# Splitting the output weights inside the attention and moving loads into the projection of a hybrid encoder layer

## What is computed

```python
h += concat(rmsnorm(y_a, g_out_a), rmsnorm(y_b, g_out_b)) @ w_out   # the mixer
h += softmax(q k^T) v @ w_xo      # q from rmsnorm(h), k and v from 256 memory rows each, w_xkv
h += hierarchical_moe(rmsnorm(h)) # 32 experts, top-1 group, top-2 experts
y  = rmsnorm(h) * g_final
```

## Time and profile before

| | |
|---|---|
| time, three runs | 1410.42 us median (1410.22 to 1417.36) |
| profiled execution | 1412.83 us, its span 1411.2 us |
| busy share of the span | TensorE 86%, VectorE 46%, ScalarE 31%, GpSimd 17% |
| granted clock, mean | 0.932 |
| chain that ended last | TensorE 73%, DMA 7%, VectorE 7%, SyncE's queue 5% |

### The profile page before, as it was taken

How to read it: one execution, slowest core, us unless ns; L and a number is a source line. 1 busy time by engine, 2 the same in 40 slices (tenths; PEclk the granted TensorE clock), 3 DMA queues, 4 the chain that set the end, 5 groups by cost and what they waited for, 6 DMA issues and landing times.

```text
span 1411.2 us, 17465 instructions
## 1 busy us (share of the span) xinstructions
PE 1208.6 (86%) x5959; PEld 938.8 (67%) x5959; DVE 647.9 (46%) x1158; ACT 437.1 (31%) x893; POOL 237.3 (17%) x350
## 2 busy tenths in 40 slices
PE   4999999599998995999989979999973998899910
PEld 3888888488877884788854445658762886667600
DVE  4433222421126775433332064435467786665257
ACT  4322222400024553211111133323110765554222
POOL 0211111100012220000000000000022352223234
PEclk9999999799999998999989999999985999999965
DMA  7211111233166114533210100004145899999676
GB/s 234 70 59 54 59 59 30 66 75 76 30 138 183 27 24 143 179 88 89 59 60 0 59 1 15 16 16 135 45 132 177 292 333 314 337 338 332 189 281 257
DMA packets 167885, 178.91 MB, mean 127 GB/s; under 512 B 39054, under 2 KB 131214, under 8 KB 167822
## 3 DMA queue, kind: packets, MB, share of 16 engines
q1 hardware_dynamic: 150350, 140.33, 33.3%
q0 software_dynamic: 13824, 31.48, 6.2%
q10 hardware_dynamic: 3648, 6.29, 1.5%
HBM read 150.48 MB, written 42.51 MB: 137 GB/s over the span
## 4 chain that ended last, share of the span: by engine, by line
PE 73%; DMA 7%; DVE 7%; SPq 5%; issue 4%; ACT 3%; POOL 1%; ACTq 0%; POOLq 0%; DVEq 0%
PE bank L420 14%; PE bank L422 13%; PE bank L421 13%; PE bank L1698 13%; PE bank L1602 3%; PE bank L1778 3%; DMA at<-in_w_exp_down 3%; PE bank L1582 3%; PE bank L1591 2%; PE bank L1744 2%; PE bank L1764 1%; PE bank L1537 1%; PE bank L1658 1%; PE bank L1707 1%; DVE at L1481 1%
## 5 line engine op out<-in xcount | busy, mean ns | idle before, releaser
L420 PE MATMUL bank<-at,at 128*128 128x512 f32 (+1 forms) x1024 | 389.5, 380 | 27.2 <-DVE at L415 17.3
L422 PE MATMUL bank<-at,at 128*128 128x512 f32 (+1 forms) x1024 | 378.6, 370 | 0.0
L421 PE MATMUL bank<-at,at 128*128 128x512 f32 (+1 forms) x1024 | 378.3, 369 | 0.0
L415 DVE TENSOR_TENSOR at<-at,at 128x1024 fp32r<-128x1024 f32 (+2 forms) x106 | 156.9, 1484 | 182.9 <-ACT at L410 170.9
L420 PEld LDWEIGHTS bank<-at,at 128*128 128x128 f32 x1024 | 199.3, 195 | 61.2 <-DVE at L415 21.3
L422 PEld LDWEIGHTS bank<-at,at 128*128 128x128 f32 x1024 | 198.4, 194 | 31.8
L421 PEld LDWEIGHTS bank<-at,at 128*128 128x128 f32 x1024 | 199.6, 195 | 29.5
L1698 PE MATMUL bank<-at,at 128*128 128x512 f32 (+1 forms) x560 | 186.2, 491 | 6.0 <-DVE at L1222 3.3
L410 ACT ACTIVATE at<-at 128x1024 fp32r<-128x1024 f32 (+3 forms) x106 | 130.4, 1266 | 135.7 <-DMA at<-in_w_exp_down 38.9
L1698 PEld LDWEIGHTS bank<-at,at 128*128 128x128 f32 x560 | 93.6, 195 | 91.1 <-issue 86.3
L688 POOL TENSOR_TENSOR at<-at 128x1 f32<-128x1 f32 x88 | 27.9, 317 | 724.9 <-ACT at L980 332.9
(11 more groups left out here) (168 smaller groups left out, 1302.6 us busy)
## 6 DMA issues: line engine op xcount, KB each, us to landing
at<-in_w_exp_gate SPq DMA_DIRECT2D x39, 512.0 KB
at<-in_w_exp_up SPq DMA_DIRECT2D x39, 512.0 KB
at<-in_w_exp_down SPq DMA_DIRECT2D x39, 512.0 KB
at<-y_tok SPq DMA_DIRECT2D x24, 512.0 KB, 9.2
at<-y_mix SPq DMA_DIRECT2D x12, 512.0 KB, 4.5
xn_moe<-at SPq DMA_DIRECT2D x12, 512.0 KB, 2.6
at<-in_w_in SPq DMA_DIRECT2D x2, 2048.0 KB, 12.2
at<-in_x_sample POOLq DMA_DIRECT2D x8, 512.0 KB, 3.9
```

Of the source, the lines that this page charges most:

```text
L415: nc.vector.tensor_tensor(lo, x, hi.bitcast(F32), ALU.subtract).then_inc(lo_made, 1)
L420: nc.tensor.matmul(out, w_hi, x_hi, start=(k == 0), stop=False)
L421: nc.tensor.matmul(out, w_lo, x_hi, start=False, stop=False)
L422: last = nc.tensor.matmul(out, w_hi, x_lo, start=False, stop=(k == len(terms) - 1))
```

## The change

Three things are moved.

1. w_out is split in 16 pieces of 128 x 512, eight within steps of pair 1 (first half) and eight within steps of pair 3 (second half). Before pair 1 ScalarE waits for all 16 pieces of w_out. The buffers are laid out anew for it.
2. The rows of tiles 0 and 1 are loaded in pair 3 after the store of its third group, in place of the end. Their squares, their scaling, the transposes of tile 0 and their evacuation are put into the last steps of that pair. The last pair is written out in every stream.
3. The rows of tiles 2 and 3 are loaded right after the last stores. The k half of w_xkv (2 MB) is issued between the rows of tiles 3 and 4, its v half between those of 5 and 6, the memory rows between 7 and 8, and the router weights behind w_xq at the end of the projection.

```diff
@@ sync @@
             for g in range(NKG):
                 store_group(0, g)
                 for part in range(3 * g, min(3 * g + 3, 2 * KT)):
                     load_w_out(part)
...
-            for g in range(NKG - 1):
-                store_group(NPAIR - 1, g)
+            for g in range(3):
+                store_group(NPAIR - 1, g)
             for j in range(2):
                 sp.wait_ge(ya_stored[j], 16 * 2 * NT // 2)
             sp.wait_ge(na_stored[0], 32 * (3 * (NPAIR - 1) + 1))
-            sp.wait_ge(s_biased, 2 * NPAIR * NSTEP)
             for j in range(2):
-                load_rows(0, j, a["x_prompt"][0][0:GTOK])
-            store_group(NPAIR - 1, NKG - 1)
+                load_rows(0, j)
+            for g in range(3, NKG):
+                store_group(NPAIR - 1, g)
             for j in range(2):
                 sp.wait_ge(na_stored[j], 16 * 2 * NPAIR * NKG // 2)
-            sp.dma_start(w_xkv, a["w_xkv"][0].rearrange("(k p) n -> p k n", p=P)).then_inc(w_kv_rt_xo_here, 16)
-            sp.dma_start(w_rt[:, :, 0:NG], a["w_router_group"][0].rearrange("(k p) n -> p k n", p=P)).then_inc(w_kv_rt_xo_here, 16)
-            sp.dma_start(w_rt[:, :, NG:], a["w_router_expert"][0].rearrange("(k p) n -> p k n", p=P)).then_inc(w_kv_rt_xo_here, 16)
+            for j in range(2):
+                load_rows(1, j)
+            sp.dma_start(w_xk, w_xkv[:, :, 0:HALF]).then_inc(w_kv_xo_here, 16)
+            for j in range(2):
+                load_rows(2, j)
+            sp.dma_start(w_xv, w_xkv[:, :, HALF:]).then_inc(w_kv_xo_here, 16)
+            for j in range(2):
+                load_rows(3, j)
             for n, rows in enumerate((a["mem_prompt"][0], a["mem_sample"][0])):
                 for j in range(2):
                     sp.dma_start(mem_in[2 * n + j], rows[j * P:(j + 1) * P]).then_inc(mem_here[j], 16)
-            for j in range(2):
-                load_rows(1, j, a["x_prompt"][0][GTOK:2 * GTOK])
-            with sp.Fori(2, NT // 2) as i:
+            for i in range(4, NT // 2):
+                for j in range(2):
+                    load_rows(i, j)
             sp.wait_ge(wo_done, NT)
+            sp.dma_start(w_xq, a["w_xq"][0].rearrange("(k p) n -> p k n", p=P)).then_inc(w_xq_rt_here, 16)
+            sp.dma_start(w_rt[:, :, 0:NG], a["w_router_group"][0].rearrange("(k p) n -> p k n", p=P)).then_inc(w_xq_rt_here, 16)
+            sp.dma_start(w_rt[:, :, NG:], a["w_router_expert"][0].rearrange("(k p) n -> p k n", p=P)).then_inc(w_xq_rt_here, 16)
@@ scalar @@
                     if s >= 1:
                         evac_pT(s - 1)
+                    if hp in (1, NPAIR - 1) and s < KT:
+                        n = int(hp == NPAIR - 1)
+                        make_hi(act, split_w_out(n, s), w_out_hi[n][:, s], w_out[n][:, s])
+                    if hp == NPAIR - 1 and s in (NSTEP - 3, NSTEP - 2):
+                        square_y(0, s - (NSTEP - 3))
...
+            head_pair(0)
             act.wait_ge(w_out_here, 16 * 2 * KT)
-            make_hi(act, split_w_out(0), w_out_hi[0], w_out[0])
+            for hp in range(1, NPAIR):
+                head_pair(hp)
             split_y_tile(0, 0)
@@ vector @@
+                    if hp == NPAIR - 1 and s == NSTEP:
+                        evac_yT(0, 0)
                     if 1 <= s <= NSTEP:
                         evac_pT(s - 1)
+                    if hp in (1, NPAIR - 1) and 1 <= s <= KT:
+                        n = int(hp == NPAIR - 1)
+                        make_lo(dve, split_w_out(n, s - 1), w_out_lo[n][:, s - 1], w_out[n][:, s - 1], w_out_hi[n][:, s - 1])
                     if s >= 2:
                         evac_o(s - 2)
+                    if hp == NPAIR - 1 and s in (NSTEP - 2, NSTEP - 1):
+                        scale_y(0, s - (NSTEP - 2))
@@ tensor @@
+                    if isinstance(hp, int) and hp == NPAIR - 1 and s == NSTEP:
+                        pe.wait_ge(s_biased, 2 * (base + NSTEP - 1))
+                        transpose_y(0, 0)
                     if 1 <= s <= NSTEP:
                         transpose_p(s - 1)
```

More of the change, by code:

```diff
@@ L128, in hymba_encoder @@
         w_out = [at(48 + 16 * n, KT, HALF) for n in range(2)]
-        w_out_hi = [at(kb, KT, HALF, dt=F32R) for kb in (80, 128)]
+        w_out_hi = [at(kb, KT, HALF, dt=F32R) for kb in (80, 168)]
         w_out_lo = [at(48 + 16 * n, KT, HALF, dt=F32R) for n in range(2)]
[L131 to L135, removed]
+        y_cat = [at(144 + 4 * j, D) for j in range(2)]
+        x_res = [at(96 + 4 * j, D) for j in range(2)]
+        y_T = [at(116 + 4 * j, KT, P) for j in range(2)]
+        y_hi = [at(kb, KT, P, dt=F32R) for kb in (202, 104)]
+        y_lo = [at(116 + 4 * j, KT, P, dt=F32R) for j in range(2)]
         yb_junk = at(200, HALF)
-        mem_in = [at(kb, D) for kb in (120, 124, 184, 188)]
-        w_xkv = at(144, KT, D)
+        mem_in = [at(kb, D) for kb in (108, 112, 184, 188)]
+        w_xk, w_xv = at(128, KT, HALF), at(152, KT, HALF)
         mem_T = at(64, KT, 4 * P)
-        k_mem = at(128, XH, 4 * P)
-        v_mem = at(136, 4, HALF)
+        k_mem = at(96, XH, 4 * P)
+        v_mem = at(104, 4, HALF)
         hs = [at(194 + 4 * j, D) for j in range(2)]
@@ L235, in hymba_encoder @@
             sem(n) for n in ("pt_done", "pt_evac_s", "pt_evac_v", "o_done", "o_evac"))
-        w_out_here, w_kv_rt_xo_here, w_xq_here = (sem(n) for n in ("w_out_here", "w_kv_rt_xo_here", "w_xq_here"))
+        w_out_here, w_kv_xo_here, w_xq_rt_here = (sem(n) for n in ("w_out_here", "w_kv_xo_here", "w_xq_rt_here"))
         y_here, xr_here = pair("y_here"), pair("xr_here")
@@ L392, in split_w_qk, with split_w_out @@
             return 4 + NT + NCH + 2 * i + j
-        def split_w_out(n):
-            return 4 + NT + NCH + NH + 2 * n
+        def split_w_out(n, k):
+            return 4 + NT + NCH + NH + KT * n + k
         def split_y(t):
-            return 4 + NT + NCH + NH + (1 if isinstance(t, int) and t == 0 else 2 + t)
+            return 4 + NT + NCH + NH + 2 * KT + t
         SPLIT_W_XO = split_y(NT - 1) + 1
@@ L560, in _, with load_rows @@
                 head_pair(hp)
-            for g in range(NKG - 1):
-                store_group(NPAIR - 1, g)
-            def load_rows(i, j, x_rows):
-                if not (isinstance(i, int) and i == 0):
+            def load_rows(i, j):
+                if i > 0:
                     sp.wait_ge(yt_done[j], i)
-                sp.dma_start(y_cat[j], y_mix[bass.ds((2 * i + j) * P, P)]).then_inc(y_here[j], 16)
-                if not (isinstance(i, int) and i == 0):
+                sp.dma_start(y_cat[j], y_mix[(2 * i + j) * P:(2 * i + j + 1) * P]).then_inc(y_here[j], 16)
+                if i > 0:
                     sp.wait_ge(h_added[j], 2 * i)
-                x_rows = x_rows.rearrange("(r n c) d -> n c r d", n=4, c=QC)
+                x_rows = a["x_prompt"][0] if i < SEQ_P // GTOK else a["x_sample"][0]
+                row0 = (i if i < SEQ_P // GTOK else i - SEQ_P // GTOK) * GTOK
+                x_rows = x_rows[row0:row0 + GTOK].rearrange("(r n c) d -> n c r d", n=4, c=QC)
                 for n in range(2):
                     sp.dma_start(x_res[j][n * HD:(n + 1) * HD], x_rows[2 * j + n]).then_inc(xr_here[j], 16)
+            for g in range(3):
+                store_group(NPAIR - 1, g)
             for j in range(2):
@@ L937, in split_y_tile @@
                 make_hi(act, split_y(t), y_hi[j], y_T[j])
-            for j in range(2):
-                square_y(0, j)
+            head_pair(0)
             act.wait_ge(w_out_here, 16 * 2 * KT)
-            make_hi(act, split_w_out(0), w_out_hi[0], w_out[0])
+            for hp in range(1, NPAIR):
+                head_pair(hp)
             split_y_tile(0, 0)
[L944 to L947, removed]
             def out_tile(i, j, last, last_pair):
@@ L1232, in split_y_tile @@
                 make_lo(dve, split_y(2 * i + j), y_lo[j], y_T[j], y_hi[j])
[L1234 to L1237, removed]
+            for hp in range(NPAIR):
+                head_pair(hp)
             split_y_tile(0, 0)
-            make_lo(dve, split_w_out(1), w_out_lo[1], w_out[1], w_out_hi[1])
             def add_rows(i, j, last, last_pair):
@@ L1667, in _ @@
                         if h == 0:
-                            pe.wait_ge(w_kv_rt_xo_here, 48)
+                            pe.wait_ge(w_kv_xo_here, 32)
                         pe.wait_ge(nt_evac, 2 * 4)
-                        steps = [(w_xkv[:, k, h * P:(h + 1) * P], mem_T[:, k]) for k in range(KT)]
+                        steps = [(w_xk[:, k, h * P:(h + 1) * P], mem_T[:, k]) for k in range(KT)]
                     elif kind == "v_mem":
                         m = which[0]
-                        steps = [(mem_T[:, k, m * P:(m + 1) * P], w_xkv[:, k, HALF:]) for k in range(KT)]
+                        steps = [(mem_T[:, k, m * P:(m + 1) * P], w_xv[:, k]) for k in range(KT)]
                     elif kind == "q":
```

(2 more changed lines are left out.)

22 lines of the change are left out of this document (8 added, 14 removed).

## The result

| | before | changed |
|---|---|---|
| median | 1411.88 us (6 runs, 1409.77 to 1417.36) | 1423.86 us (6 runs, 1421.86 to 1429.55) |
| ratio | | 1.0082, 95% interval 1.0055 to 1.0110 |
| profiled execution, span | 1411.2 us | 1422.3 us |
| granted clock, mean | 0.932 | 0.932 |

The change made the kernel slower by 0.8%. In a second set of runs, made later, the same kernel came to 1.0058 (1.0044 to 1.0073). The two intervals overlap, so the 0.25% between the sets isn't clear of noise.

The account below looks back on a forecast made before the run. TensorE bounds attention and projection; between them lie 20.8 us in which it works 3.9. Sum: 1411.2 - 21.0 + 7.3 + 4.9 + 0 + 19.8 = 1422.2, on the median about 1421; 8-in-10 range 1403 to 1427.

Parts of the forecast that it names:

- The wait for w_out: Start of pair 1: ScalarE waits 5.65 us for the last piece; with slow clock 7.3 us, bounds 5.4 to 8.
- The pieces: Pairs 1 and 3: 16 pieces of w_out's split cost 2.45 us a pair, 4.9 for two; bounds 0 to 10.9.
- Rows inside the last pair: Last pair: ScalarE waits 1.7 us for tile 1's rows, TensorE covers it; cost 0, uncovered 1 to 3 us.
- The start of the projection: First product 17.4 us earlier, 1.5 us less slow clock, 2.1 us stall of tile 2 gone; gain 21.0 us.
- tile 2's stall: Projection of the kernel before: TensorE idle 2.1 us for tile 2's rows; claimed to go, gain 2.1 us.
- The stalls: Projection: y_cat of tiles 4, 6, 8 queued behind large loads; three stalls of 4.1 us, with slow clock 19.8 us.
- the slower rate: Projection: load rate taken from w_xq's 2 MB in 8.5 us; 3 MB then take 9.5 + 2.1 us.
- Rival (a): Projection: large loads hold up less, stalls of 2.0 to 3 us, clock kept; about 1410 us, chance 0.27.
- Rival (b): Projection: y_cat of tiles 4, 6 and 8 not held up beyond the 1.0 us to spare; 1401.6 us, chance 0.16.
- Rival (c): Last pair doesn't hold the work: splits cost 10.9 us, projection starts 3 us later; 1430 us, chance 0.07.

## Why the prediction was right

The forecast of 1421 us, 0.75% slower, held; measured were 0.8% in the first set and 0.6% in the second. By its steps:

- **The wait for w_out** (7.3): measured 7.6, by the pair's length with and without it. The landing at about 458.1 and the fall of the clock came as reckoned; it was found from SyncE's order and a wait on ScalarE, neither of which shows in the kernel before as a cost.
- **The pieces** (2.45 a pair): measured 0.88 in the second pair; for the last pair no run measures them. This is the term that was most off, 4.9 for about 1.8. The prediction took what each step exceeds VectorE's idle time by as paid. The run with twice the pieces shows that the first eight operations are mostly hidden and the next eight mostly paid. I read that as a lag of VectorE which the other engines' work ahead takes up until it is used up; no run shows the lag itself.
- **Rows inside the last pair** (0, or 1 to 3): the place is right, ScalarE does wait for y_cat of tile 1. Together with the pieces the pair is 2.3 to 3.8 us longer, against 2.45 predicted for the pieces alone; the wait is 0 to 1.5 of it, by when the rows land (1.5 in the first trace, where 0 was forecast). What the prediction left out is a further 1.4 us, likely the transposes of tile 0, which aren't all free.
- **The start of the projection** (17.4, and 1.5 for the clock and 2.1 for tile 2's stall): from last values to first product 18.9 less by the trace. Of the 3.8 that the last pair is longer, 0.9 are booked under the pieces and 1.5 under the rows; the other 1.4 belong here. That leaves 17.5 for 17.4.
- **The stalls** (three of 4.1, with 2.5 of slow clock each, 19.8): measured three of 4.97, 4.76 and 4.49 with 2.3 each, 21.0 together; the other traces of this order have up to 23.8. Less the 1.5 and 2.1 that the projection of the kernel before had of its own this is 17.4, and the projection did get 17.2 longer. y_cat was there 11.9 us after x_res of tile 3 went out, and the slower rate had given 9.5 + 2.1; I had shaded the stall by half a microsecond towards the faster. The 2.1 us of latency in that rate don't follow from the two loads that the prediction names: a line through 13.1 us for 4 MB and 8.5 for 2 MB has 3.9 us and 4.6 for each 2 MB, by which the 3 MB are an estimated 10.8 us. The 11.9 that were measured lie nearer to the sum that was made.

The total is nearer than its terms. Against the forecast's 11.0 more the trace has 11.1, but the pieces came out about 3.1 lower, the rows 1.5, the stalls 1.2 and all behind the projection 1.1 higher, and the smaller terms add up to -0.6. That these cancel is luck; that two large costs would stand against one large gain, where, and within about 20% how large, is not.

Rival (a), shorter stalls with the clock kept, falls in the changed kernel; in the kernel with the 1 MB pieces, five of six rests, of 0.3 to 3.2 us, did keep it. Rival (b), that the loads are hidden, falls by the 10 us landing. Its time, 1401.6, is near that of the kernel in which the order is mended (1403.5; its projection has no stall), which again holds in the total only, with the pieces too dear. Rival (c) didn't occur: the pieces cost 0.9 in the second pair, and the first product starts 7.2 us earlier in the span than in the kernel before.

What stays open is the 1.1 us behind the projection, and which of the smaller terms scatter between sets of runs. Two sources are visible in the traces, below.

## What to carry to other kernels

Where one queue issues all loads, a load's place matters more than its cover: find, for each small load that an engine waits for every turn, how much there is to spare (here 1.0 us a tile), and put large loads behind the small one, not ahead of it. A piece of work that is moved away may have been the cover of something else; here the split of w_out had covered 6 MB. And a wait set for the whole of a tensor takes the time of its last piece, so see when that goes out.

## What the runs showed of the hardware

The length of a rest doesn't decide alone what TensorE's clock does. It read 0.5 within the first microsecond or so of work after every rest of 4.5 us and more that was looked at. In the projection it kept 1.0 through rests of 1.6, 1.8, 2.07, 2.86 and 3.21 us, and fell after one of 3.03. Two rests stand in all kernels here and go both ways:

- The wait for v_att in the first head pair. The eight values behind it took 1.13 us after rests of 1.72 and 3.13 to 3.78 us (five traces), and 2.0 after rests of 2.96 to 3.39 (six traces). The last values of that pair started at 446.8 to 448.5 where the clock was kept and at 449.1 to 451.2 where it was lost.
- The first transposes behind the projection, after a rest of 2.13 us in all eleven traces. Their 16 took 1.94 us in five of them and 3.0 to 3.6 in the other six; the next transposes then started 0.3 to 0.9 us later. The changed kernel has both:

```profile
723.56 3.55 PE L1661 MATMUL bank<-at,at 128*128 128x128 f32 x16 [2.13 <-DVE at L1272]
...
722.12 1.94 PE L1661 MATMUL bank<-at,at 128*128 128x128 f32 x16 [2.13 <-DVE at L1272]
```

The first row is from its first trace, the second from its second. Such rests are thus sources of scatter between executions whose code is the same there; what decides which way they go, no run here shows.

A load of 512 KB behind 2 MB on the same queue landed within 8.1 to 10.1 us of its issue, three times in the changed kernel. The 16 KB load of the earlier trace rows, which took 13.2 us behind the 4 MB of w_xkv, stands behind the 2 MB of w_xq in the new order: in the run with y_cat one tile ahead it took 8.5 us, w_xq itself 8.3. So its time follows what is ahead of it, and isn't that of its own short rows. The Trainium skill's page "DMA: Bandwidth & Descriptors", section "Queues, rings and completion order", has each engine take a row's descriptors in ring order; the landing times agree with it. Its fit in "Anatomy of one DMA", 2.0 us and 436 GB/s, would have put y_cat of tile 4 an estimated 9.2 us behind the issue of x_res of tile 3; it took 11.9.
